# A streaming transformer layer in one kernel: the first stage's products ahead of their norms, the selection norms one head earlier, and the two ends of the down phase reordered

## The chip, the cores and the metric

The kernel runs on one core of one Trainium2 chip. The metric is the device time of one execution in microseconds (us), the median of several runs. Names: PE is the matmul engine (PEld its weight loads), DVE the vector engine, ACT the scalar engine, POOL is GpSimd, SP the engine that issues most loads. "ACTq" and "SPq" are their instruction queues, here the issuing of DMAs.

## The reference, cut to what matters

T = 544 tokens (512 of a prompt, 32 of a running stream), 2048 features. One layer: three mixers share an input projection, a merge follows, then a feed-forward part (PEER) that picks 16 of 16,384 experts in each of 8 heads.

```python
def rmsnorm(x, g):
    xf = x.astype(jnp.float32)
    y = xf * lax.rsqrt(jnp.mean(xf * xf, axis=-1, keepdims=True) + EPS) * g.astype(jnp.float32)
    return y.astype(x.dtype)

def memory_kv(mem, g_mem, w_kv):                 # mem: 256 tokens
    k, v = jnp.split(rmsnorm(mem, g_mem) @ w_kv, 2, axis=-1)
...
gq, gk, gv, gr, ga, sq, sk, sv, mq, gates = in_proj(rmsnorm(x, g_mix), w_in)
...
def peer(h, w_q, g_q, sub_keys, u_tab, v_tab):   # h = rmsnorm(x2, g_ffn)
    q = rmsnorm((x @ w_q).reshape(T, PEER_HEADS, PEER_QDIM), g_q)
    sc = jnp.einsum('thpd,hpkd->thpk', q, sub_keys)
    s_top, i_top = lax.top_k(sc, PEER_TOPK)      # 16 of 128, for both halves
    ...                                          # 16 of the 256 sums; softmax gives the gates
    a = jnp.einsum('td,tkd->tk', xt, u)
    c = gt * jax.nn.gelu(a, approximate=False)
    return jnp.einsum('tk,tkd->td', c, vsel)
...
y = rmsnorm(x2 + peer(...), g_final)
```

## The kernel before

**Numbers in two parts.** PE multiplies in a rounded form of fp32, so each operand is split: `hi`, rounded, and `lo`, what is left. A product is hi x hi + hi x lo + lo x hi, three matmuls for each chunk of 128 features.

**The ring of weight pieces.** Weights come as pieces of 128 x 1024 (512 KB) in the order of use. A ring of four slots (`RING`) holds each piece three times: `w_raw`, loaded by SP (`load_piece`, L188), `w_hi` and `w_lo`, both made by POOL (`split_piece`, L198: a rounding, then a subtraction). PE uses a piece in `use_piece` (L214); `piece_used` frees its slot. SP may load piece i when piece i - 4 is split, POOL split it when piece i - 4 is used.

**Norms.** Activations lie with features on partitions, so a norm's sum of squares is a matmul with a matrix of ones (`Norm.add_square`, L299), after ACT's squares. Then ACT takes the root (`root`), DVE the reciprocal (`invert`) and, for each chunk of 128 features, the product with gain and reciprocal root (L333); ACT rounds it to `hi` and DVE subtracts for `lo` (`scale`, L321).

**Stages.** Each stage is a block of five engine programs, and all engines meet at its end. The first is `stage_memory_kv`: it norms the 256 memory tokens and multiplies them with 32 pieces, two for each of 16 output blocks. Beside them ACT squares x, a chunk a block, and PE sums it. `stage_input_projection` reloads x, scales it, and multiplies it with 117 blocks of two pieces. At the end of a stage POOL splits the four pieces with which the next begins.

**Selection** (`stage_select`). Each of 8 heads has six "up" blocks on PE (`up.tensor`; the products of the experts' first table), which do not depend on the head and fill the time. `up.scalar` evicts them through a Gelu on ACT. Their results alternate between two PSUM banks, and a block may start when the one two before it is evicted. A head itself runs: queries loaded, squared (ACT), summed (PE), root (ACT), reciprocal and two scalings (DVE), one up block meanwhile; 20 score matmuls (PE), copied by ACT; then a long chain on DVE for the 16 best (`max1` ... `idx2`), the 256 candidates (`cand`), the best of these, `over`, ACT's exponential, and `gate`.

**The down phase** (`stage_experts`). 32 sets (`G`), each of four rows of keys. DVE weighs the up results with the gates (`weigh`, L2340), ACT rounds (L2318), DVE subtracts (`rest`, L2345); the terms of a set are prepared during the set before. PE makes 16 blocks (`j`) of a set in four PSUM banks, DVE adds each to `y` in SBUF (L2362). The last 128 tokens are treated apart: POOL gathers a row of the table for each slot and DVE adds it (`add_down`), five to a set. In the last set PE also sums the squares of the finished blocks for the final norm, whose scaled chunks are stored as they come.

## Time and profile before

| | before |
|---|---|
| time, median of 3 runs (lowest to highest) | 5435.06 us (5430.29 to 5442.83) |
| the profiled execution's own time, and its span | 5435.13 us, 5433.3 us |
| granted clock of PE, mean over the span | 0.973 |
| PE matmul busy | 5161.4 us (95%) |
| DVE busy | 2467.3 us (45%) |
| ACT busy | 830.0 us (15%) |
| POOL busy | 3489.8 us (64%) |
| moved by DMA | 1011 MB, 186 GB/s |

The span runs from the first to the last instruction of the profiled execution. The granted clock is the share of PE's full clock of 2.4 GHz that it was given, 0.50 or 1.00 at any moment. Matmuls are pipelined, and a busy PE is not PE at its peak. In a timeline the bracket is the idle time of the engine before the instruction, and what ended it.

### The profile page before, as it was taken

How to read it: one execution, taken by the hardware profiler on the slowest of the kernel's cores; microseconds unless marked ns; L12 is line 12 of the kernel's file. 1: busy time of each engine (PE TensorE's matmuls, PEld its weight loads, DVE VectorE, ACT ScalarE, POOL GpSimd, SP SyncE). 2: the span in 40 equal slices, each digit the busy share in tenths (PEclk: the TensorE clock that was granted, in tenths of full speed). 3: DMA queues.
4: the chain of work that ended last, by engine and by line, in shares of the span. 5: the costliest groups of instructions: out<-in, count | busy, mean ns of one | idle time of the engine just before them, and what ended most of it. 6: DMA issues, size and time to landing. Idle time of an engine off the chain costs nothing. (4 is left out here: it accounts for less than half of the span.)

```text
span 5433.3 us, 90535 instructions
## 1 busy us (share of the span) xinstructions
PE 5161.4 (95%) x33434; PEld 5007.2 (92%) x33434; DVE 2467.3 (45%) x3782; ACT 830.0 (15%) x1318; POOL 3489.8 (64%) x2072
## 2 busy tenths in 40 slices
PE   8899999999999889989999999999998899999998
PEld 8899999999989776989898889999998899999998
DVE  1200000012211243430207777888885788888854
ACT  2100000023322333100101111212211000000001
POOL 7555555544444232555456777888887799999974
PEclk9999999999999989999999999999999999999999
DMA  5333333333232443652323334988897888888852
GB/s 195 130 113 110 109 111 110 117 105 108 83 122 101 146 149 113 214 179 82 119 105 131 122 126 147 327 322 323 323 334 258 318 309 301 311 308 301 301 170 95
DMA packets 344224, 1011.39 MB, mean 186 GB/s; under 512 B 39632, under 2 KB 133680, under 8 KB 308288
## 3 DMA queue, kind: packets, MB, share of 16 engines
...
q14 instruction: 77, 0.63, 0.0%
HBM read 883.11 MB, written 126.76 MB: 186 GB/s over the span
## 5 line engine op out<-in xcount | busy, mean ns | idle before, releaser
L208 POOL TENSOR_TENSOR w_lo<-w_raw,w_hi 128x1024 fp32r<-128x1024 f32 x906 | 2216.9, 2447 | 168.5 <-POOL w_hi L204 167.2
L204 POOL TENSOR_SCALAR w_hi<-w_raw 128x1024 fp32r<-128x1024 f32 x906 | 1003.7, 1108 | 1676.2 <-PE ps L232 1453.5
L228 PE MATMUL ps<-h_hi,w_hi 128*128 128x272 f32 (+1 forms) x6816 | 1740.8, 312 | 85.2 <-DVE h_lo L321 34.5
L232 PE MATMUL ps<-h_hi,w_lo 128*128 128x272 f32 (+1 forms) x6816 | 1718.2, 309 | 0.0
L230 PE MATMUL ps<-h_lo,w_hi 128*128 128x272 f32 (+1 forms) x6816 | 1708.3, 308 | 0.0
L228 PEld LDWEIGHTS ps<-h_hi,w_hi 128*128 128x128 f32 x6816 | 1144.4, 190 | 111.1 <-issue 105.4
L230 PEld LDWEIGHTS ps<-h_lo,w_hi 128*128 128x128 f32 x6816 | 1144.1, 190 | 6.4
L232 PEld LDWEIGHTS ps<-h_hi,w_lo 128*128 128x128 f32 x6816 | 1138.0, 190 | 2.8
L228 PE MATMUL ps<-ex_c_hi,w_hi 128*128 128x416 f32 x2048 | 720.0, 352 | 34.8 <-DVE ex_c_lo L2345 34.5
L232 PE MATMUL ps<-ex_c_hi,w_lo 128*128 128x416 f32 x2048 | 723.7, 353 | 0.0
L230 PE MATMUL ps<-ex_c_lo,w_hi 128*128 128x416 f32 x2048 | 715.7, 349 | 0.0
L1307 DVE SCALAR_TENSOR_TENSOR swa_sb_s<-ps,swa_sb_bias 128x384 f32<-128x384 f32 (+2 forms) x32 | 16.2, 508 | 1191.5 <-PE ps L1156 1191.5
L228 PEld LDWEIGHTS ps<-ex_c_hi,w_hi 128*128 128x128 f32 x2048 | 385.1, 188 | 38.5 <-issue 36.1
L2362 DVE TENSOR_TENSOR ex_y<-ps,ex_y 128x416 f32<-128x416 f32 x512 | 296.4, 584 | 223.6 <-PE ps L232 220.1
L230 PEld LDWEIGHTS ps<-ex_c_lo,w_hi 128*128 128x128 f32 x2048 | 385.5, 188 | 6.6
L232 PEld LDWEIGHTS ps<-ex_c_hi,w_lo 128*128 128x128 f32 x2048 | 384.6, 188 | 2.3
L1850 DVE SCALAR_TENSOR_TENSOR g_sb_u_rows<-g_sb_u_rows,ps 128x2048 f32<-128x2048 f32 x128 | 291.8, 2280 | 118.9 <-DMA g_sb_u_rows<-peer_u,sp_expert 118.8
L1862 DVE SCALAR_TENSOR_TENSOR ps<-ex_v_rows,sp_coef,ps 128x2048 f32<-128x2048 f32 x127 | 297.8, 2345 | 25.5 <-DMA ex_v_rows<-peer_v,sp_expert 25.5
L2175 DVE TENSOR_SCALAR g_sb_rows<-const_sb,sp_turned 128x128 f32<-128x128 f32 x416 | 301.9, 726 | 3.8 <-PEq L1873 3.8
L2318 ACT ACTIVATE ex_c_hi<-ex_c 128x416 fp32r<-128x416 f32 x128 | 70.4, 552 | 1068.9 <-DVE ex_c L2340 972.8
L2345 DVE TENSOR_TENSOR ex_c_lo<-ex_c,ex_c_hi 128x416 fp32r<-128x416 f32 x128 | 206.3, 1613 | 3.4 <-ACT ex_c_hi L2318 3.4
L2340 DVE TENSOR_TENSOR ex_c<-ex_up,ex_gate 128x416 f32<-128x416 f32 x128 | 173.5, 1358 | 25.3 <-DMA ex_gate<-gate 25.3
...
## 6 DMA issues: line engine op xcount, KB each, us to landing
...
up<-up_out ACTq DMA_DIRECT2D x128, 208.0 KB, 3.3
...
```

Source lines behind the costliest of these rows:

```text
L204: pool.tensor_scalar(self.whi[:, slot, :], self.raw[:, slot, :], 1.0, 1.0, ALU.mult, ALU.mult).then_inc(self.hi_done, 1)
L208: pool.tensor_tensor(self.wlo[:, slot, :], self.raw[:, slot, :], self.whi[:, slot, :].bitcast(F32), ALU.subtract).then_inc(self.split_done, 1)
L228: pe.matmul(acc, hi, x, start=first, stop=False)
L230: pe.matmul(acc, hi, x, start=False, stop=False)
L232: mm = pe.matmul(acc, lo, x, start=False, stop=last)
L1850: dve.scalar_tensor_tensor(row_of_slot, row_of_slot, 1.0, self.token_rows, ALU.mult, ALU.mult, accum_out=self.dot[:, s:s + 1]).then_inc(se ...
L1862: dve.scalar_tensor_tensor(self.token_rows, buf[:, s % GATHERS, :], c, self.token_rows, ALU.mult, ALU.add).then_inc(self.summed, 1)
L2175: dve.tensor_scalar(rows[:, group % 2, t, :], iota, of(0), of(2), ALU.is_equal, ALU.mult)
L2318: act.activation(c_hi[:, s, :], c_all[:, c, :], ACT.Copy).then_inc(hi_done, 1)
L2340: dve.tensor_tensor(by_tile(c_all[:, c, :]), by_tile(up[:, parity, c, :]), gate[:, parity, :, c * G_TILE:(c + 1) * G_TILE], ALU.mult).then ...
L2345: dve.tensor_tensor(c_lo[:, VSET * (G % 2) + c, :], c_all[:, c, :], c_hi[:, VSET * (G % 2) + c, :].bitcast(F32), ALU.subtract).then_inc(lo ...
L2362: dve.tensor_tensor(y[:, j, 0:TD], ps[:, 4 + j % 4, 0:TD], y[:, j, 0:TD], ALU.add).then_inc(added, 1)
```

## The change

The memory stage. The operand of the product is the memory times the gain, without the norm; DVE writes it to PSUM, ACT rounds it from there, DVE subtracts. The squares are added up by DVE in PSUM, one matmul with ones sums them over partitions after the third piece, and each output block is multiplied by the reciprocal root when DVE evicts it. The memory is loaded in four parts, with weight piece 0 behind the first. From piece 4 on ACT rounds the weight pieces of this stage, and POOL only subtracts (`rest_of_piece`). The norm of x is made whole in this stage: squares in blocks 0 to 5, the sum after block 6, root and reciprocal in block 7, and two chunks scaled in each of blocks 7 to 14, with x loaded a second time for them. The input projection neither loads nor scales.

Selection. The squares of head h + 1 are made after head h's first up block, summed after its second, the root taken after that; DVE scales the queries between head h's second indices and its candidates; the scores of h + 1 follow head h's sixth up block. Sums and scores of head 0 stand ahead of all up blocks. ACT's exponential of head h moves from behind its fifth eviction to behind its third.

The down phase. Only the first set's terms are loaded at first; SP loads y when they have landed, ACT the next two sets' terms behind its first roundings. The first set's preparation of the second moves to blocks 10 to 14, and the gathers and their adds start one set later. In the last set DVE adds the squares, and PE sums them once, after its last block.

```diff
+    def rest_of_piece(self, pool, slot, i):
+
+        if needed(i - RING + 1):
+            pool.wait_ge(self.piece_used, i - RING + 1)
+        pool.wait_ge(self.hi_done, i + 1)
+        held(pool)
+        pool.tensor_tensor(self.wlo[:, slot, :], self.raw[:, slot, :],
+                           self.whi[:, slot, :].bitcast(F32), ALU.subtract).then_inc(self.split_done, 1)
...
 
...
+        product = lambda b: core.ps[:, 7 if b == 2 else b % 2, 0:N_MEM]
+        tmp = lambda k: core.ps[:, 2 + k % 2, 0:N_MEM]
+        added = total = core.ps[:, 6, 0:N_MEM]
+        sq = lambda k: x[:, k, :]
+        x_sq = lambda k: halves_of(x_part[:, k % (2 * FOUR), :])
+        x_added, x_total, x_rstd = core.acc_view(2), core.acc_view(1), core.acc_view(3)
+        x_tmp = lambda k: core.acc_view(1 + k % 2)
+        x_squares_of = lambda b: range(SQUARES * b, min(SQUARES * (b + 1), KD))
+        x_scaled_of = lambda b: range(2 * (b - X_SCALE), 2 * (b - X_SCALE) + 2) if 0 <= b - X_SCALE < KD // 2 else ()
...
+            part = lambda n: slice(FOUR * n, FOUR * n + FOUR)
+            sp.dma_start(core.gain[:, :], io["gain"]).then_inc(gain_loaded, 16)
+            sp.dma_start(x[:, part(0), :], io["mem"][:, part(0), :]).then_inc(x_loaded[0], 16)
+            core.load_piece(sp, 0, AT_MEM)
+            for n in range(1, KD // FOUR):
+                sp.dma_start(x[:, part(n), :], io["mem"][:, part(n), :]).then_inc(x_loaded[n], 16)
+            for n in range(1, RING):
+                core.load_piece(sp, n, AT_MEM + n)
             sp.dma_start(core.const[:, :], io["const"]).then_inc(core.const_loaded, 16)
-            sp.dma_start(core.gain[:, :], io["gain"]).then_inc(core.const_loaded, 16)
-            core.load_pieces(sp, AT_MEM, AT_IN + RING)
+            core.load_pieces(sp, AT_MEM + RING, AT_IN + RING)
-            core.split_pieces(pool, AT_MEM, AT_IN + RING)
+            core.split_pieces(pool, AT_MEM, POOL_FIRST)
+            for i in range(POOL_FIRST, PIECES_MEM):
+                core.rest_of_piece(pool, i % RING, i)
+            core.split_pieces(pool, AT_IN, AT_IN + RING)
...
+            for b in range(MEM_BLOCKS):
+                if b > 2:
+                    pe.wait_ge(kv_ready, b - 1)
+                for piece in range(2):
+                    i = AT_MEM + 2 * b + piece
+                    core.use_piece(pe, i % RING, i, [
+                        ([product(b)], [hi[:, k, :]], [lo[:, k, :]], k == 0, k == KD - 1,
+                         (lo_ready, k + 1) if b == 0 else None, None)
+                        for k in range(PIECE_K * piece, PIECE_K * (piece + 1))])
+                    if i == AT_MEM + 2:
+                        pe.wait_ge(core.const_loaded, 16)
+                        pe.wait_ge(sq_added, KD)
+                        pe.matmul(total, core.ones, squares[:, :], start=True, stop=True).then_inc(sum_ready, 1)
+                if b == X_SUM:
+                    pe.wait_ge(x_sq_added, KD)
+                    for out, (t0, n) in zip(core.acc(1), HALVES):
+                        mm = pe.matmul(out, core.ones, x_squares[:, t0:t0 + n], start=True, stop=True)
+                    mm.then_inc(sum_ready, 1)
...
+            def round_piece(i):
+                act.wait_ge(core.hi_done, i)
+                act.wait_ge(core.raw_loaded[i % RING], 16 * (i // RING + 1))
+                act.wait_ge(core.piece_used, i - RING + 1)
+                act.activation(core.whi[:, i % RING, :], core.raw[:, i % RING, :], ACT.Copy).then_inc(core.hi_done, 1)
+
+            def square_x(k):
+                n = k // FOUR
+                act.wait_ge(x_part_loaded[n % 2], 16 * (n // 2 + 1))
+                act.activation(x_sq(k), x_sq(k), ACT.Square).then_inc(x_sq_ready, 1)
+            for k in range(KD):
+                act.wait_ge(tmp_ready, k + 1)
+                act.activation(hi[:, k, :], tmp(k), ACT.Copy).then_inc(hi_ready, 1)
+                act.activation(sq(k), x[:, k, :], ACT.Square).then_inc(sq_ready, 1)
+            for b in range(MEM_BLOCKS):
+                for piece in range(2):
+                    if POOL_FIRST <= 2 * b + piece + RING < PIECES_MEM:
+                        round_piece(2 * b + piece + RING)
...
+                    if piece == 0:
+                        for k in x_squares_of(b):
+                            square_x(k)
...
+                        for k in x_scaled_of(b):
+                            act.wait_ge(x_scaled, k + 1)
+                            act.activation(halves_of(h_hi[:, k, :]), x_tmp(k), ACT.Copy).then_inc(x_hi_ready, 1)
...
+                if b == 0:
+                    act.wait_ge(core.const_loaded, 16)
+                    act.wait_ge(sum_ready, 1)
+                    act.activation(std[:, :], total, ACT.Sqrt, bias=core.eps,
+                                   scale=1.0 / D_MODEL).then_inc(std_ready, 1)
+                act.wait_ge(kv_ready, b + 1)
+                act.dma_start(row(io["mem_kv"], b), kv[:, b % 2, :]).then_inc(kv_stored[b % 2], 16)
...
+            for k in range(KD):
+                dve.wait_ge(x_loaded[k // FOUR], 16)
+                if needed(k - 1):
+                    dve.wait_ge(lo_ready, k - 1)
+                dve.tensor_scalar(tmp(k), x[:, k, :], mem_gain(k), None, ALU.mult).then_inc(tmp_ready, 1)
+                if k:
+                    rest(k - 1)
+            rest(KD - 1)
...
+            for k in range(KD):
+                add(k, added, sq(k), squares[:, :], sq_ready, sq_added)
...
+            for b in range(MEM_BLOCKS):
+                for k in x_squares_of(b):
+                    add(k, x_added, x_sq(k), halves_of(x_squares[:, :]), x_sq_ready, x_sq_added)
+                if b == 0:
+                    dve.wait_ge(std_ready, 1)
+                    dve.reciprocal(rstd[:, :], std[:, :]).then_inc(rstd_ready, 1)
+                    dve.wait_ge(rstd_ready, 1)
+                if needed(b // 2):
+                    dve.wait_ge(kv_stored[b % 2], 16 * (b // 2))
+                dve.wait_ge(core.piece_used, AT_MEM + 2 * b + 2)
+                dve.tensor_tensor(kv[:, b % 2, :], product(b), rstd[:, :], ALU.mult).then_inc(kv_ready, 1)
+                if b == X_SCALE:
+                    dve.wait_ge(std_ready, 2)
+                    dve.reciprocal(x_rstd, halves_of(x_std[:, :])).then_inc(rstd_ready, 1)
+                    dve.wait_ge(rstd_ready, 2)
+                for k in x_scaled_of(b):
+                    n = KD // FOUR + k // FOUR
+                    dve.wait_ge(x_part_loaded[n % 2], 16 * (n // 2 + 1))
+                    if needed(k - 1):
+                        dve.wait_ge(x_lo_ready, k - 1)
+                    dve.scalar_tensor_tensor(x_tmp(k), halves_of(x_part[:, k % (2 * FOUR), :]), mix_gain(k), x_rstd, ALU.mult,
+                                             ALU.mult).then_inc(x_scaled, 1)
+                    if k:
+                        x_rest(k - 1)
+            x_rest(KD - 1)
...
-            norm.copies(act)
...
-            norm.scale(dve)
...
-            def head(h):
+            def sums(h):
                 pe.wait_ge(act_s.sem, act_s.at("sq", h))
+            def scores(h):
                 pe.wait_ge(keys_loaded, 16 * (h + 1))
...
-                for n in range(1, UP_HEAD):
+
+            def head(h, last=False):
+                for n in range(2):
                     up.tensor(pe, UP_HEAD * h + n, n)
-            rounds(pe, PEER_HEADS, head)
-
-            pe.wait_ge(dve_s.sem, dve_s.at("gate", PEER_HEADS - 1))
+                if not last:
+                    sums(h + 1)
+                for n in range(2, UP_HEAD):
+                    up.tensor(pe, UP_HEAD * h + n, n)
+                if not last:
+                    scores(h + 1)
+            sums(0)
+            scores(0)
+            rounds(pe, PEER_HEADS - 1, head)
+            head(PEER_HEADS - 1, last=True)
...
+                pair = UP_HEAD // 2 * h
                 if not last:
-
                     load(h + 1)
-                for n in range(1, UP_HEAD - 1):
-                    up.scalar(act, UP_HEAD // 2 * h + n // 2, n % 2)
-                act.wait_ge(dve_s.sem, dve_s.at("over", h))
+                up.scalar(act, pair, 0)
+                if not last:
+                    square(h + 1)
+                up.scalar(act, pair, 1)
+                if not last:
+                    root(h + 1)
+                up.scalar(act, pair + 1, 0)
+                act.wait_ge(dve_s.sem, dve_s.at("over", h) - (normed if last else 0))
                 held(act)
-                act.activation(e[:, :, :], over[:, :, :], ACT.Exp).then_inc(*act_s.did("e"))
-                up.scalar(act, UP_HEAD // 2 * h + (UP_HEAD - 1) // 2, 1)
+                act.activation(e[:, :, :], over[:, :, :], ACT.Exp).then_inc(*(
+                    (act_s.sem, 1) if last else act_s.did("e")))
+                for n in range(3, UP_HEAD):
...
+                if last:
+                    dve_s.skip("rstd", "qn0", "qn1")
+                else:
+                    normalize(h + 1)
...
+    FIRST_ADDS = 1
+    WEIGH_AT = {j: (c,) for c, j in enumerate((0, 2, 4, 6))}
+    REST_AT = {j: (c,) for c, j in enumerate((8, 9, 11, 12))}
+    FIRST_WEIGH_AT, FIRST_REST_AT = {10: (0, 1), 11: (2, 3)}, {13: (0, 1), 14: (2, 3)}
...
         def _(sp):
+            sp.wait_ge(terms_loaded[0], 32)
+            for n in range(4):
+                sp.dma_start(y[:, 4 * n:4 * n + 4, :], rows("x2")[:, 4 * n:4 * n + 4, :]).then_inc(y_loaded[n], 16)
-                while s < SLOTS and (s < GATHERS or add_piece(s - GATHERS) + 2 <= i - AT_DOWN - RING):
+                while s < SLOTS and add_piece(s - GATHERS) + 2 <= i - AT_DOWN - RING:
...
-                    if isinstance(G, int) and G == LAST and piece:
-                        for k in (2 * piece - 2, 2 * piece - 1):
-                            norm.add_square(pe, k, k % 2, k == 0, False)
...
-            for k in (KD - 2, KD - 1):
-                norm.add_square(pe, k, k % 2, False, k == KD - 1)
+            pe.wait_ge(norm.sq_used, KD)
+            for out, (t0, n) in zip(norm.sum, norm.halves):
+                mm = pe.matmul(out, core.ones, squares[:, t0:t0 + n], start=True, stop=True)
+            mm.then_inc(squares_summed, 1)
...
-            for n in range(4):
-                act.dma_start(y[:, 4 * n:4 * n + 4, :], rows("x2")[:, 4 * n:4 * n + 4, :]).then_inc(y_loaded[n], 16)
-            load_terms(1)
+                if G == 0:
+                    load_terms(1)
...
-            norm.scalar(act)
+            act.activation(norm.std[:, 0:1], core.eps, ACT.Sqrt)
+            for k in range(KD):
+                norm.square(act, k)
+            act.wait_ge(squares_summed, 1)
+            norm.root(act)
...
+            def add_square(k):
+                dve.wait_ge(norm.sq_ready, k + 1)
+                if k == 1:
+                    dve.tensor_tensor(squares[:, :], norm.sq[:, 0, :], norm.sq[:, 1, :],
+                                      ALU.add).then_inc(norm.sq_used, 2)
+                    return
+                dve.wait_ge(norm.sq_used, k)
+                dve.tensor_tensor(squares[:, :], squares[:, :], norm.sq[:, k % 2, :],
+                                  ALU.add).then_inc(norm.sq_used, 1)
...
+                    elif j % 4 == 0:
+                        dve.wait_ge(y_loaded[j // 4], 16)
                     dve.tensor_tensor(y[:, j, 0:TD], ps[:, 4 + j % 4, 0:TD], y[:, j, 0:TD],
                                       ALU.add).then_inc(added, 1)
-                    if G < LAST and j in (0, 2, 4, 6):
-                        weigh(G + 1, j // 2)
-                    if G < LAST and j in (8, 9, 11, 12):
-                        rest(G + 1, (8, 9, 11, 12).index(j))
-                    if j % 3 == 1 and s < SLOTS:
+                    if G < LAST:
+                        for c in (WEIGH_AT if G else FIRST_WEIGH_AT).get(j, ()):
+                            weigh(G + 1, c)
+                        for c in (REST_AT if G else FIRST_REST_AT).get(j, ()):
+                            rest(G + 1, c)
+                    elif j >= 2:
+                        add_square(j - 1)
+                    if j % 3 == 1 and s < SLOTS and G >= FIRST_ADDS:
                         sparse.add_down(dve, buf, s)
...
+            add_square(KD - 1)
             norm.vector(dve, out=y)
```

## Rows read from the trace of the kernel before

**Rows 1.** Groups by line, 50 to 146 us: count | busy us, mean ns | idle before

```profile
L208 POOL TENSOR_TENSOR w_lo<-w_raw,w_hi 128x1024 fp32r<-128x1024 f32 x28 | 67.0, 2394 | 5.1 <-POOL w_hi L204 5.1
...
L204 POOL TENSOR_SCALAR w_hi<-w_raw 128x1024 fp32r<-128x1024 f32 x27 | 28.4, 1052 | 0.0
```

**Rows 2.** Timeline of PE, memory stage: start us, duration us, engine, line

```profile
134.00 0.35 PE L228 MATMUL ps<-mem_hi,w_hi 128*128 128x256 f32 x1
...
136.94 1.08 PE L304 MATMUL ps<-in_sq,const_sb 128*128 128x272 f32 x4
```

**Rows 3.** Timeline of the start, POOL and PE

```profile
11.89 1.04 POOL L204 TENSOR_SCALAR w_hi<-w_raw 128x1024 fp32r<-128x1024 f32 x1 [11.44 <-DMA w_raw<-weights]
...
27.44 0.55 PE L228 MATMUL ps<-mem_hi,w_hi 128*128 128x256 f32 x1 [4.64 <-DVE mem_lo L321]
```

**Rows 4.** Timeline from the memory stage into the input projection

```profile
146.17 1.16 PE L304 MATMUL ps<-in_sq,const_sb 128*128 128x272 f32 x4 [0.94 <-ACT in_sq L466]
...
152.91 2.34 POOL L208 TENSOR_TENSOR w_lo<-w_raw,w_hi 128x1024 fp32r<-128x1024 f32 x1 [0.18 <-POOL w_hi L204]
...
155.55 2.04 SPq L498 DMA_DIRECT2D in_x<-x  x4
...
163.00 0.79 PE L228 MATMUL ps<-h_hi,w_hi 128*128 128x272 f32 x2 [15.68 <-DVE h_lo L321]
...
188.44 0.63 ACT L537 ACTIVATE in_stage<-ps 128x544 f32<-128x544 f32 x1 [2.02 <-PE ps L232]
```

**Rows 5.** Timeline of selection, ACT and PE

```profile
2869.78 0.52 ACT L1813 ACTIVATE up_out<-ps 128x416 f32<-128x416 f32 x1 [8.54 <-PE ps L232]
...
2900.85 3.97 PE L1917 MATMUL ps<-sel_sb_sq,const_sb 128*128 128x272 f32 x8 [4.00 <-ACT sel_sb_sq L1953]
...
2914.77 2.58 PE L1927 MATMUL ps<-sel_sb_keys,sel_sb_qn 128*128 128x128 f32 x20 [0.44 <-DVE sel_sb_qn L2000]
```

**Rows 6.** The score matmuls, by their line

```profile
L1927 PE MATMUL ps<-sel_sb_keys,sel_sb_qn x160: 272/275/348, 2848.8 to 3313.5; 128*128 128x128 f32 x128, 128*32 128x128 f32 x32
```

**Rows 7.** Timeline of selection, DVE, one head

```profile
2984.97 2.03 DVE L2006 MAX8 sel_sb_top<-sel_sb_sc 128x8 f32<-128x128 f32 x10 [4.36 <-ACT sel_sb_sc L1965]
...
2997.42 1.47 DVE L2028 TENSOR_TENSOR sel_sb_cand<-sel_sb_top 128x1280 f32<-128x1280 f32 x1
...
3010.97 5.98 DVE L2072 TENSOR_TENSOR sel_sb_hot<-sel_sb_rank,const_sb 128x1280 f32<-128x1280 f32 x2
...
3026.66 0.77 DVE L2093 TENSOR_TENSOR sel_sb_chosen<-sel_sb_e,sel_sb_inv 128x80 f32 x1 [0.24 <-DVE sel_sb_inv L2090]
...
3039.49 3.55 DVE L1995 RECIPROCAL sel_sb_rstd<-sel_sb_std 128x544 f32<-128x544 f32 x1 [12.06 <-ACT sel_sb_std L1956]
```

**Rows 8.** Timeline of the start of the down phase

```profile
4204.24 9.52 ACTq L2310 DMA_DIRECT2D ex_y<-x  x1
...
4224.31 2.10 DVE L2340 TENSOR_TENSOR ex_c<-ex_up,ex_gate 128x416 f32<-128x416 f32 x4 [22.64 <-DMA ex_gate<-gate]
...
4232.22 0.69 PE L228 MATMUL ps<-ex_c_hi,w_hi 128*128 128x416 f32 x1 [34.49 <-DVE ex_c_lo L2345]
```

**Rows 9.** There: us; busy PE, PEld, DVE, ACT, POOL; clock; DMA; GB/s

```profile
4210.00:4220.00 10.00, 0.00 (x0) 0.00 (x0) 0.00 (x0) 0.00 (x0) 0.00 (x0) 0.50 1.02 414
```

**Rows 10.** Timeline of DVE in the last set

```profile
5406.77 0.59 DVE L2362 TENSOR_TENSOR ex_y<-ps,ex_y 128x416 f32<-128x416 f32 x1 [3.52 <-PE ps L232]
...
5409.04 0.59 DVE L2362 TENSOR_TENSOR ex_y<-ps,ex_y 128x416 f32<-128x416 f32 x1 [1.68 <-PE ps L232]
```

**Rows 11.** Groups of instructions by line, DVE, whole span

```profile
L2362 DVE TENSOR_TENSOR ex_y<-ps,ex_y 128x416 f32<-128x416 f32 x512 | 296.4, 584 | 223.6 <-PE ps L232 220.1 <-issue 1.8
...
L2345 DVE TENSOR_TENSOR ex_c_lo<-ex_c,ex_c_hi 128x416 fp32r<-128x416 f32 x128 | 206.3, 1613 | 3.4 <-ACT ex_c_hi L2318 3.4
...
L2000 DVE SCALAR_TENSOR_TENSOR sel_sb_qn<-sel_sb_q,gain_sb,sel_sb_rstd 128x544 f32<-128x544 f32 x16 | 27.2, 1740 | 1.9 <-DVE sel_sb_rstd L1995 1.9
...
L1859 DVE TENSOR_SCALAR ps<-ex_v_rows,sp_coef 128x2048 f32<-128x2048 f32 x1 | 2.3, 2339 | 0.0
```

243 lines of the change are left out of this document (122 added, 121 removed).

## The prediction

> **What bounds the kernel now.** The page comes first: the matmul engine (PE) is busy for 95% of the span, so only its idle stretches, its stretches at the low clock, and the one stage in which its "busy" hides a wait are worth anything. I then read the clock and busy time by stretches, and after that the timelines of the four places that the diff touches. An edit is worth what it does to PE, or to what follows PE's last matmul.
>
> The start is poor: up to 27.4 us PE has no product to work on [rows 3], and it stands again between 147.3 and 163 [rows 4]. While it stands it is granted 0.50 of 2.4 GHz [rows 9]. Between them PE reads as full, but one piece of 24 matmuls takes 2.94 us (134.00 to 136.94), and four sums of squares of 1.08 together follow every second piece [rows 2]. GpSimd (POOL) needs 2.39 + 1.05 + 0.18 = 3.62 us for a piece [rows 1], against PE's 2.94 + 0.54. So in the memory stage POOL is the bound.
>
> **Part 1, the memory stage.** Now PE's first product starts at 27.4, though the first weights had landed by 11.9 [rows 3]. After the change the product needs no norm: DVE multiplies by the gain, ACT rounds, DVE subtracts, and the norm divides the product later. The transfers ahead of weight piece 0 fall from 2.7 MB to 0.6 MB; 3.2 MB had landed by 11.9, so 1.1 MB should land by about 6 (an estimate), and POOL's 3.6 us put PE's start near 9.8. But POOL splits the first four pieces alone (ready near 10, 16, 19, 23, as pieces 1 to 3 queue behind three parts of x), and ahead of its fourth piece PE waits for the sum of squares: 16 operand chunks at about 0.85 us a chunk, then 16 dependent additions at 0.55 each, an estimate from 0.58 for 416 elements [rows 11]. That ends at 7.9 + 13 + 8.8 = 29.6. From there 29 pieces at 2.92 are 84.7; I add 2.5 for matmuls at the low clock, 0.8 for the second sum and 1.4 for a stall at block 7, where DVE inverts the second root (3.55 for such a reciprocal [rows 7]) ahead of the copies that hold ACT's next rounding. The stage's last piece ends at 119. Now it ends at 147.3 [rows 4].
>
> POOL's part of a piece falls to 2.6, ACT's rounding is about 1.0 more, and both lie behind PE: a freed slot has three pieces (8.8 us) until it is wanted. In blocks 7 to 14 ACT rounds the odd piece only after two copies that wait for DVE, about 3.5 us after PE ends the block: 3.5 + 1.0 + 2.6 = 7.1, so 1.7 us of cover is left. If that goes, each such block costs what it lacks. DVE's new work has a PSUM operand everywhere, and such work does not stretch beside POOL: 0.58 us for 416 elements with one input in PSUM, but 1.61 with both in SBUF [rows 11].
>
> **Part 2, into the input projection.** Now x is reloaded and scaled here, and block 0 is evicted at 188.4 [rows 4]. POOL ends at 155.25, the next stage's first DMA goes at 155.55 [rows 4]: the boundary itself costs some 0.3 us. After, PE finds its operands ready, but POOL must still split the four pieces that the next stage begins with. Piece 31 leaves POOL about 4.5 us before PE's end, and four times 3.6 later POOL is done 9.8 us behind it. Block 0 is then out at 119 + 10.2 + 12.0 (this stage's block) + 2.4 (low clock) = 143.6. Parts 1 and 2 save 188.4 - 143.6 = **45**; bounds 34 (the loop of ring slots loses 11) and 53 (sum and boundary each cheaper by 4). The eight loads of x stay eight, now all on ACT's queue. The wait for the stored keys moves to the end of SP's queue, where nothing stands behind it.
>
> **Part 3, selection.** At each of seven head boundaries PE sits idle for 4.00 us until ACT has squared the next queries, and then works at the low clock, 3.97 us for 8 sums [rows 5]; the same kind of sums at full clock cost 3.52 - 1.68 = 1.84 [rows 10]. The pitch of a head is (3313.5 - 2.4 - 2848.8)/7 = 66.0, from the first and the last start of the score matmuls [rows 6], of which a head's 20 take 2.5 to 2.6 [rows 5]. Without the wait it is six blocks of 0.52 + 8.54 = 9.06 [rows 5], 1.84 for the sums and 2.5 for the scores: 58.7. Seven heads save 51. Head 0 pays: its block 0 used to cover the chain root, reciprocal, two scalings, and now follows it; 3.55 [rows 7], two scalings of 0.8 beside an idle POOL to 1.74 on average [rows 11] and some 0.7 for the root make about 6.5, with 1 for the clock. Net 44.
>
> What is late next? DVE has 12.45 us from its first maximum to the candidates, 13.55 from there to "over", and 15.7 + 0.8 on to the gates [rows 7]. Counted from the end of a head's scores, DVE finishes the second indices at 14.0 and waits for the next root until 22.1 (two blocks, the sums, a Gelu, a table load, the root); reciprocal and scalings end at 29.5, "over" at 43.1, the gates at 59.5. The next head's scores are ready for DVE at 60.3, so DVE keeps up by 0.8. ACT now waits for "over" before it may evict block 3: exponential and two table loads later this is out at 46.6, and PE wants that bank for block 5 at 47.2. A margin of 0.6 us on seven heads: I charge 1 in all. **Part 3: 43**; bounds 25 (each head loses 2.5) and 46.
>
> **Part 4, start of the down phase.** ACT issues the first terms at about 4204 and then stands 9.5 us on one load of y; DVE gets the terms at 4224.3, PE starts at 4232.2 after 34.5 idle [rows 8]. Now nothing but the first terms (1.7 MB) is in flight: y waits for them, the gathered rows come a set later. At the 414 GB/s that the queues moved then [rows 9] they are 4.1 us; with the start of a transfer and the gates' short runs I take 7, an estimate, so 4211, and 4.6 for four weighings and four remainders beside free engines: PE at 4215.6, 16.6 earlier. SP's y now stands ahead of weight pieces 4 to 7: by PE's need of piece 4 (7 + 3 x 4.5 later, 4236) some 11 MB must have moved, about what this rate gives (13 in 32 us); I charge 1.5. And set 1's weighings come two at blocks 10 and 11, its remainders two at 13 and 14: 0.58 + 2 x 1.61 = 3.8 a block [rows 11] against PE's 2.27, so DVE is 3 us late when PE wants set 1. **Part 4: 12**; bounds 4 and 17.
>
> **Part 5, the last norm.** The last set loses seven pairs of sums on PE at 1.84 each (the wait before the add alternates 3.52, 1.68 [rows 10]): **13**. DVE adds the squares instead, 15 of them under PE's 2.27 a block, with four banks of slack. These additions have two SBUF inputs. I take no stall on PE, as a set has so far held eight such instructions (1.61 for a remainder) and five gathered additions without one. Behind the last add, one addition more against a table load less: zero, within 1. Bounds 9 and 14.
>
> A rule of the Trainium skill bears on this (SBUF — State Buffer, "Who interferes with whom"): a DVE instruction with two SBUF inputs contends with a GpSimd instruction that reads SBUF, and the later one waits for all of the other. The trace agrees: 1.61 against 0.58 [rows 11]. By the rule the eight or so additions beside POOL's last pieces would each wait up to 2.4, and the sum would lose at most 3 of the 13.
>
> Sum: 45 + 43 + 12 + 13 = 113. The profiled execution took 5435.1 (span 5433.3 and 1.8 around it), and the median of the runs is 5435.06: **5322**.
>
> **Rivals.** (a) ACT's wait for "over" costs PE 2 to 3 us a head and its clock as well: 18 to 20 back, **5341**. For it: the margin of 0.6; against: DVE's times repeat well.
> (b) The loop of slots fails in the first stage, ACT's copies holding back the rounding: 8 blocks at 1.5, and POOL's last four pieces later too: **5336**.
> (c) y and terms 1 and 2 starve PE of weights in the first set: part 4 falls to nothing, **5334**. For it: the DMA engines are the bound there.
> (d) The gain multiplication contends with POOL after all: it reads SBUF alone. Sixteen instructions that wait a mean 1.2 put the sum of squares 15 to 19 later: **5339**. Against: the one such instruction with its result in PSUM took 2.34 for 2048 elements beside POOL's work [rows 11], an element a cycle with no wait. The Trainium skill (VectorE: DVE Perf Modes, "Why PSUM operands drop a tier") says that any PSUM operand bars the two-port mode; the trace agrees.
> (e) Slower: DVE becomes selection's bound. If the eight wide DVE instructions of a head each wait a whole subtraction of POOL's (2.4) more than now, the pitch grows by 19: 7 x 19 - 113 = +20, **5455**. It decides from 16 us a head. Against: these instructions were measured beside POOL already; only the scalings move.
>
> **Numbers.** Forecast 0.55, (a) 0.15, (b) 0.10, (c) 0.08, (d) 0.05, (e) 0.02, and 0.05 for two of (a) to (d) together, which would end near 5360. About 0.2%, 11 us, is what a measurement of this kernel can tell from no change. The low bounds of all parts give 5435 - 34 - 25 - 4 - 9 = 5363, the high ones 5435 - 53 - 46 - 17 - 14 = 5305. The range is 5300 to 5365. Faster 0.96, same 0.01, slower 0.03.
>
> **What would show it.** After: PE's first product near 10 with a wait of some 6 us before its fourth piece; the memory stage's last piece near 119 and POOL idle in it; block 0 evicted near 144; heads at a pitch of 59 and no wait for the squares; DVE idle some 8 us before the reciprocal; PE restarting 18 us after its last up block; the last set free of sums. Wrong would be a pitch over 61, a memory stage of over 3.1 us a piece, or a wait for weights in the first down set.

## The result, and the profile after

The changed kernel takes 5340.3 us (median of 4 runs, 5333.5 to 5347.0) against 5436.8 for the kernel before on the same chip; the ratio is 0.9812, interval 0.9800 to 0.9824, so 96 to 109 us less. Forecast was 5322. Two executions, both of the run with the three edits together, took longer (5423.3 and 10176.1 us) and are left out of its median. The profiled execution has a span of 5338.1 against 5433.3, 95.2 less. Its page says of the engines:

```profile
PE 5102.9 (96%) x33252; PEld 4964.4 (93%) x33252; DVE 2513.0 (47%) x3845; ACT 848.1 (16%) x1331; POOL 3462.1 (65%) x2044
```

PE's busy time falls by 58 us, the sums of squares among it; the other 37 were idle. The work itself, weight pieces and experts, is unchanged, and so the way to read the change is stretch by stretch between events that both traces have:

| from, to | before, us | after, us | saved | forecast |
|---|---|---|---|---|
| start, first eviction of the input projection | 188.4 | 142.1 | 46.3 | 45 |
| on to selection's first sum of squares | 2646.6 | 2646.6 | 0.0 | 0 |
| selection, to the first transposition of the gates stage | 529.6 | 493.0 | 36.6 | 43 |
| gates stage, to the last up eviction | 833.2 | 842.4 | -9.2 | 0 |
| on to the first add of down set 1 | 75.3 | 65.4 | 9.9 | 12 |
| sets 1 to 30 | 1090.8 | 1090.3 | 0.5 | 0 |
| last set, first add to last add | 45.1 | 34.0 | 11.1 | 13 |
| last add to the end | 24.3 | 24.4 | -0.1 | 0 |

**The start.** Timeline of the start (start us, us, engine, line; in brackets the idle time before and its releaser), which answers to [rows 3]:

```profile
7.14 1.04 POOL L217 TENSOR_SCALAR w_hi<-w_raw 128x1024 fp32r<-128x1024 f32 x1 [6.70 <-DMA w_raw<-weights]
...
11.01 0.55 PE L250 MATMUL ps<-mem_hi,w_hi 128*128 128x256 f32 x1 [11.01 <-DVE mem_lo L538]
```

Weight piece 0 is there at 7.1, not at 11.9, and PE starts at 11.0, not at 27.4. The sum of squares comes after the third piece:

```profile
28.85 0.42 DVE L554 TENSOR_TENSOR mem_squares<-ps,mem_x 128x256 f32<-128x256 f32 x1
...
29.42 1.19 PE L474 MATMUL ps<-mem_squares,const_sb 128*128 128x256 f32 x2 [5.34 <-DVE mem_squares L554]
```

It starts at 29.42, which was forecast as 29.6, and PE stands 5.3 us for it. PE's last piece of the stage ends at 117.6 (127.87, the next stage's first matmul, less 10.28 of waiting), and POOL's fourth split of the next stage's pieces ends at 127.2. This answers to [rows 4].

**Selection.** The timeline of ACT in one head, which answers to [rows 5]:

```profile
2884.60 0.72 ACT L2069 ACTIVATE sel_sb_std<-ps,const_sb 128x544 f32<-128x544 f32 x1
...
2893.68 0.52 ACT L1909 ACTIVATE up_out<-ps 128x416 f32<-128x416 f32 x1
...
2907.46 1.28 ACT L2095 ACT_TABLE_LOAD   x1 [13.26 <-DVE sel_sb_over L2198]
2908.76 0.27 ACT L2095 ACTIVATE sel_sb_e<-sel_sb_over 128x80 f32<-128x80 f32 x1
2909.04 1.28 ACT L1909 ACT_TABLE_LOAD   x1
2910.34 0.52 ACT L1909 ACTIVATE up_out<-ps 128x416 f32<-128x416 f32 x1
...
2911.79 0.52 ACT L1909 ACTIVATE up_out<-ps 128x416 f32<-128x416 f32 x1 [0.94 <-ACT up_out L1909]
```

The root is taken at 2884.6, between the second and the third eviction. PE does not wait for it; DVE does, 8.37 us in this head (next rows), which the prediction expected ("some 8 us"). Then ACT stands 13.3 us for DVE's "over", loads two tables around the exponential, and evicts block 3 only at 2910.34. Block 4 is evicted right behind it. What DVE did in that time (answers to [rows 7]):

```profile
2885.55 3.55 DVE L2119 RECIPROCAL sel_sb_rstd<-sel_sb_std 128x544 f32<-128x544 f32 x1 [8.37 <-ACT sel_sb_std L2069]
...
2892.87 2.33 DVE L2160 TENSOR_TENSOR sel_sb_cand<-sel_sb_top 128x1280 f32<-128x1280 f32 x1
...
2906.27 1.08 DVE L2198 TENSOR_TENSOR sel_sb_over<-sel_sb_best 128x80 f32<-128x80 f32 x1
2907.28 5.08 DVE L2204 TENSOR_TENSOR sel_sb_hot<-sel_sb_rank,const_sb 128x1280 f32<-128x1280 f32 x2
```

"cand" takes 2.33 where it took 1.47, and "over" ends at 2907.35, 44.1 us after the copy of the head's scores begins (2863.23). The 2.33 is no scatter: "cand" took 1.47 in all eight heads before, and 2.32 or 2.33 in the first seven heads after. What differs is POOL's rounding of a weight piece. Before, it begins with "cand" or up to 0.1 us behind it, and it is POOL's rounding that takes longer (1.05 alone):

```profile
2997.43 2.38 POOL L204 TENSOR_SCALAR w_hi<-w_raw 128x1024 fp32r<-128x1024 f32 x1 [0.96 <-PE ps L232]
```

After, it begins 0.3 to 0.4 us ahead of "cand" (here at 2892.51 against 2892.87) and "cand" takes longer, and so does POOL's subtraction that follows (2.40 alone):

```profile
2892.51 1.35 POOL L217 TENSOR_SCALAR w_hi<-w_raw 128x1024 fp32r<-128x1024 f32 x1 [0.84 <-PE ps L254]
2894.04 3.42 POOL L221 TENSOR_TENSOR w_lo<-w_raw,w_hi 128x1024 fp32r<-128x1024 f32 x1 [0.18 <-POOL w_hi L217]
```

And on PE, between block 4 and block 5:

```profile
2910.06 0.35 PE L254 MATMUL ps<-h_hi,w_lo 128*128 128x416 f32 x1
2911.26 0.42 PE L250 MATMUL ps<-h_hi,w_hi 128*128 128x416 f32 x1 [0.84 <-POOL w_lo L221]
```

PE idles 0.84 us, and the start of block 5 is 1.0 us late against the 0.19 between its matmuls. The row names a weight piece of POOL as the releaser. The copies of the scores are 59.9 us apart from the second head on (2863.23, 2923.12, ...). The granted clock stays at 1.00 through all of these heads.

**The gates stage.** Nothing in it was edited. DVE's timeline near its start:

```profile
3293.04 2.29 DVE L1946 SCALAR_TENSOR_TENSOR g_sb_u_rows<-g_sb_u_rows,ps 128x2048 f32<-128x2048 f32 x1 [9.69 <-DMA g_sb_u_rows<-peer_u,sp_expert]
...
3296.42 1.84 DVE L2310 TENSOR_SCALAR g_sb_cols<-const_sb,sp_turned 128x128 f32<-128x128 f32 x1
3298.17 0.33 DVE L2309 TENSOR_SCALAR g_sb_rows<-const_sb,sp_turned 128x128 f32<-128x128 f32 x1
3298.43 2.43 DVE L2310 TENSOR_SCALAR g_sb_cols<-const_sb,sp_turned 128x128 f32<-128x128 f32 x1
```

DVE makes four one-hot pairs, a group, then waits for the first gathered rows of the table, multiplies them, and makes the next group. Two instructions that take 0.28 us elsewhere take 1.84 and 2.43 here, while POOL rounds and subtracts a piece (3297.10 to 3300.78). PE stands 5.23 us for that group:

```profile
3301.01 2.05 PE L2291 MATMUL ps<-g_sb_cols,g_sb_rows 128*128 128x128 f32 x8 [5.23 <-DVE g_sb_cols L2310]
```

**The down phase.** DVE's timeline from the first terms on (answers to [rows 8]):

```profile
4137.03 2.10 DVE L2485 TENSOR_TENSOR ex_c<-ex_up,ex_gate 128x416 f32<-128x416 f32 x4 [9.14 <-DMA ex_gate<-gate]
4139.04 2.09 DVE L2490 TENSOR_TENSOR ex_c_lo<-ex_c,ex_c_hi 128x416 fp32r<-128x416 f32 x4
4145.96 0.59 DVE L2516 TENSOR_TENSOR ex_y<-ps,ex_y 128x416 f32<-128x416 f32 x1 [4.83 <-PE ps L254]
...
4169.13 3.46 DVE L2485 TENSOR_TENSOR ex_c<-ex_up,ex_gate 128x416 f32<-128x416 f32 x2
...
4180.88 3.56 DVE L2490 TENSOR_TENSOR ex_c_lo<-ex_c,ex_c_hi 128x416 fp32r<-128x416 f32 x2
```

The terms arrive at 4137.0 and PE starts at 4141.4, after 17.5 us idle instead of 34.5. But two weighings of set 1 begin at 4169.1, the last two remainders end at 4184.4, and PE waits for them:

```profile
4184.89 0.69 PE L250 MATMUL ps<-ex_c_hi,w_hi 128*128 128x416 f32 x1 [5.04 <-DVE ex_c_lo L2490]
```

**The end**, which answers to [rows 10]:

```profile
5313.74 0.59 DVE L2516 TENSOR_TENSOR ex_y<-ps,ex_y 128x416 f32<-128x416 f32 x1 [1.04 <-PE ps L254]
...
5315.89 1.28 PE L2436 MATMUL ps<-ex_squares,const_sb 128*128 128x272 f32 x4 [2.19 <-DVE ex_squares L2499]
...
5317.95 3.55 DVE L338 RECIPROCAL last_rstd<-last_std 128x544 f32<-128x544 f32 x1 [2.12 <-ACT last_std L312]
```

The adds come every 2.27 us up to the last, within 0.05; one sum of 1.28 follows.

### The profile page after: what moved, and what is told of

It reads as the page before. It is cut to its first block and busy times, and to the rows that moved or that the text cites. A ratio compares the mean times of both kernels' runs of the same rounds, so it can differ in the third digit from the quotient of the medians.

```text
span 5338.1 us, 89996 instructions
## 1 busy us (share of the span) xinstructions
PE 5102.9 (96%) x33252; PEld 4964.4 (93%) x33252; DVE 2513.0 (47%) x3845; ACT 848.1 (16%) x1331; POOL 3462.1 (65%) x2044
## 3 DMA queue, kind: packets, MB, share of 16 engines
q10 hardware_dynamic: 142640, 215.86, 11.4%
## 5 line engine op out<-in xcount | busy, mean ns | idle before, releaser
L221 POOL TENSOR_TENSOR w_lo<-w_raw,w_hi 128x1024 fp32r<-128x1024 f32 x878 | 2157.8, 2458 | 163.4 <-POOL w_hi L217 160.9
L217 POOL TENSOR_SCALAR w_hi<-w_raw 128x1024 fp32r<-128x1024 f32 x878 | 967.9, 1102 | 1598.6 <-PE ps L254 1353.6
L2309 DVE TENSOR_SCALAR g_sb_rows<-const_sb,sp_turned 128x128 f32<-128x128 f32 x416 | 315.7, 759 | 12.0 <-PEq L1969 12.0
L637 ACT ACTIVATE in_stage<-ps 128x544 f32<-128x544 f32 x73 | 45.7, 626 | 835.0 <-PE ps L254 835.0
```

Source lines behind the costliest of these rows:

```text
L217: pool.tensor_scalar(self.whi[:, slot, :], self.raw[:, slot, :], 1.0, 1.0, ALU.mult, ALU.mult).then_inc(self.hi_done, 1)
L221: pool.tensor_tensor(self.wlo[:, slot, :], self.raw[:, slot, :], self.whi[:, slot, :].bitcast(F32), ALU.subtract).then_inc(self.split_done, 1)
L637: act.activation(halves_of(stage[:, u, :]), core.acc_view(u), func).then_inc(out_ready, 1)
L2309: dve.tensor_scalar(rows[:, group % 2, t, :], iota, of(0), of(2), ALU.is_equal, ALU.mult)
```

## The experiments

Times of whole runs scatter by some 10 us on either side of a median, so small effects are read from the stretches of the profiled executions and the ratios stand beside them. Each group of four ran on one chip with the kernel before, whose medians were 5446.0, 5445.2 and 5442.8.

### The exponential behind the fifth eviction

```diff
                 up.scalar(act, pair + 1, 0)
+                for n in range(3, UP_HEAD - 1):
+                    up.scalar(act, pair + n // 2, n % 2)
                 act.wait_ge(dve_s.sem, dve_s.at("over", h) - (normed if last else 0))
...
-                for n in range(3, UP_HEAD):
-                    up.scalar(act, pair + n // 2, n % 2)
+                up.scalar(act, pair + (UP_HEAD - 1) // 2, 1)
```

> The changed kernel with one edit: in each head of selection ACT's exponential stands behind the fifth eviction again (it waits for "over" there), not behind the third. Theory A (ACT's wait for "over" makes the eviction of a head's fourth up block late, so PE loses about 1.1 us a head at its sixth up block): the 0.84 us wait of PE in each head goes, the pitch of a head falls from 59.9 to 58.8 us, seven heads give 8 us, about 5332. Rival B (the row says what it means: POOL's weight piece is late there): the wait stays, pitch 59.9, 5340. Rival C (the exponential is then late for DVE's sum): DVE waits for it before the gates and the next head's maxima slip, pitch over 60.

Measured: 5331.6, ratio 0.9795 (0.9770 to 0.9821). Selection takes 485.7 instead of 493.0, 7.3 less, and the copies of the scores are 59.1 and 58.8 apart. ACT's timeline in the same head:

```profile
2900.56 0.52 ACT L1909 ACTIVATE up_out<-ps 128x416 f32<-128x416 f32 x1 [7.27 <-PE ps L254]
...
2909.62 0.52 ACT L1909 ACTIVATE up_out<-ps 128x416 f32<-128x416 f32 x1 [8.55 <-PE ps L254]
...
2910.91 1.28 ACT L2097 ACT_TABLE_LOAD   x1 [0.77 <-ACT up_out L1909]
2912.21 0.27 ACT L2097 ACTIVATE sel_sb_e<-sel_sb_over 128x80 f32<-128x80 f32 x1
...
2921.59 1.03 ACT L2077 ACTIVATE sel_sb_sc<-ps 128x1024 f32<-128x1024 f32 x1 [1.11 <-DVE sel_sb_inv L2223]
```

Block 3 is evicted at 2900.56, as soon as PE has made it, and PE has no idle time in the head. POOL's work was not touched, so the releaser in PE's row was the wrong name: it was ACT's late eviction (theory A). ACT's copy of the scores now waits for DVE's last work on the head (the 1.11 in the last row). But DVE still idles 7.9 us in each head before its reciprocal, and that takes the lateness up: a head of 58.8 us is PE's own work without a gap, near the 58.7 of the prediction.

### The first dot product one group later

```diff
-                for _ in range(DOTS_AFTER[group % STEPS]):
+                for _ in range(DOTS_AFTER[group % STEPS] if group else 0):
```

> The changed kernel with one edit: in the gates stage the first gathered dot product stands behind DVE's second group of one-hot rows, not behind its first. Theory A (PE's 5.2 us wait at the second group comes from DVE's order: that group stands behind a dot product that waits 9.7 us for the first gathered rows, and is then stretched beside POOL): the wait goes and with it some 2 us at the low clock; last up block less first transposition falls from 842.3 to about 835, total 5333. Rival B (the gathered rows and the shared DMA engines bound the start of the stage): the wait moves to the third group with much the same size, 842, 5340.

Measured: 5336.2, ratio 0.9796 (0.9776 to 0.9817). The gates stage takes 827.0, 15 less than after the change (7 were expected) and 6 less than before it, and the view of waits has none of PE for one-hot columns in it. The middle of the kernel, which no edit touches, took 12 us more in this execution, which hides it in the total. Theory A holds for the wait, at twice its price in this pair of executions, of which the changed one had a late landing (the table below).

### The weighings of set 1 earlier

```diff
-    FIRST_WEIGH_AT, FIRST_REST_AT = {10: (0, 1), 11: (2, 3)}, {13: (0, 1), 14: (2, 3)}
+    FIRST_WEIGH_AT, FIRST_REST_AT = {7: (0,), 8: (1,), 9: (2,), 10: (3,)}, {11: (0,), 12: (1,), 13: (2,), 14: (3,)}
```

> The changed kernel with one edit: in the first down set the four weighings of set 1 stand at blocks 7 to 10 and its remainders at 11 to 14, one a block, instead of two at 10, 11, 13, 14. Theory A (the 5.0 us wait of PE before set 1 is DVE's order alone): the wait goes and the 2 us at the low clock behind it, set 1 starts 7 us earlier, 5333. Rival B (the terms of set 1 have not landed at block 7, about 25 us after PE's start): DVE waits for the transfer, the adds to y behind it are late and PE stalls for a bank in the first set: no gain or a loss of up to 5 us, 5340 to 5345.

Measured: 5339.4, ratio 0.9809 (0.9789 to 0.9828). Set 1 ends 5.1 us earlier (72.9 against 78.0 from the first add to set 1's last), but the last set begins 1.5 us later (1135.3 against 1133.8 from the first add). The view of waits over the down phase (waiting engine and operation, releaser: us, times, longest), here:

```profile
DVE ps L1958 <- DMA ex_v_rows<-peer_v,sp_expert: 60.5, 44, 6.2
...
PE ps L250 <- DVE ex_c_lo L2490: 18.7, 2, 17.4
...
PE ps L250 <- DVE ex_y L2516: 4.6, 4, 2.1
```

and in the changed kernel:

```profile
PE ps L250 <- DVE ex_c_lo L2490: 22.5, 2, 17.5
DVE ps L1958 <- DMA ex_v_rows<-peer_v,sp_expert: 20.7, 22, 2.6
```

The terms had landed, so rival B is out, and the wait before set 1 falls from 5.0 to 1.3 (each total has the 17.5 of the start in it). The gain is gone by set 16: DVE waits 60 us for gathered rows instead of 21, and PE four times, 4.6 us, for a bank that DVE has not emptied. Whether the edit does this is not shown. The run with SBUF operands (below) has the down phase of the changed kernel, and there too DVE waited 65.3 us for gathered rows, and PE for banks.

### The three edits together

> The three edits of the other runs together on the changed kernel. Theory: the three losses are separate, each in its own stretch, so their gains add: 8 + 7 + 7 = 22 us, 5318. Rival: the start of the gates stage depends on when selection ends, so that part comes out otherwise beside the first edit; then the sum misses by the size of that wait, 5 us.

Measured: 5313.8 (5310.1 to 5327.1, the three executions that the ratio takes), ratio 0.9756 (0.9731 to 0.9781), against 0.9812 (0.9800 to 0.9824) for the changed kernel. The profiled execution is one of the two left out (its gates stage took 926 us), so its stretches are not read. By the two ratios the edits together give 30 us, and by the ends of their intervals 10 to 51: they help, but the expected 22 and the rival's 5 less can't be told apart.

### Each part alone

The kernel before, with functions of the changed one: `stage_memory_kv` and `stage_input_projection`; `stage_select`; `stage_experts` with only the start changed; `stage_experts` with only the last norm changed.

```diff
-            norm = Norm(core, norm_ctx, "in", None, KD, T, G_MIX, hi, lo, 4, core.sem("in_x_loaded"))
-            stage_memory_kv(core, norm)
-            stage_input_projection(core, hi, lo, norm)
+            stage_memory_kv(core, hi, lo, kv, kv_stored)
+            stage_input_projection(core, hi, lo, kv_stored)
```

> The kernel before with the memory stage and the input projection of the change alone. Theory A (the parts are independent, and the first stage gives all of its 46.3 us by block 0 of the input projection): block 0 evicted at 142, 46 us less than before, and every later stage as long as before. Rival B (the gain is given back, since the stages behind it start with other timings): less than 40 in the total while block 0 is at 142.

Measured: 5395.6, ratio 0.9895 (0.9876 to 0.9913). The first eviction comes at 143.4, 45.0 earlier; the unchanged middle took 8 us more in this execution. By the ratio the part gives 47 to 67 us, by its own stretch 45; nothing is seen to be given back (theory A).

> The kernel before with the selection of the change alone. Both theories: selection itself (first sum of squares to the gates stage's first transposition) falls from 529.6 to 493.0 us, with a PE wait of about 0.85 in each of seven heads. Theory A (the 9.5 us longer gates stage of the changed kernel was chance of that execution): the gates stage takes about 833 us to its last up block, total 36 less. Rival B (selection's new end makes the start of the gates stage wait): gates stage 842, PE waits 5 us for the second group, total 27 less.

Measured: 5407.1, ratio 0.9929 (0.9912 to 0.9946), span 5396.2. Selection 492.6, gates stage 835.4: theory A, 37 less.

> The kernel before with the start of the down phase of the change alone, the last norm as before. Theory: PE restarts 17.5 us after its last up block instead of 34.5, then waits 5 us before set 1 and works 2 us more at the low clock: 17.0 - 7.2 = 10 less in total. Rival (the later gathered adds end beyond their old place and cost what the start gives): sets 24 to 30 longer by some us, less than 5 in total.

Measured: 5429.9, ratio 0.9967 (0.9954 to 0.9979). PE's first down product stands 17.2 us behind the start of the last up eviction instead of 34.4, and from there to the first add of the last set it is 1140.2 instead of 1131.7: 17.1 - 8.5 = 8.6 less, near the 10 expected. The ratio says more, 11 to 25 us.

> The kernel before with the last norm of the change alone. Theory A (six pairs of sums leave the last set, the seventh ran behind PE's last block anyway): last set's adds 45.1 us apart from first to last before, 34.0 after, total 11.1 less. Rival B (the seventh pair counts too, as forecast): 13 less, tail 1.8 shorter.

Measured: 5430.1, ratio 0.9976 (0.9963 to 0.9989). The last set takes 36.3 from last add to last add instead of 47.4, 11.1 less (theory A).

By their own stretches the four parts give 45.0, 37.0, 8.6 and 11.1, together 101.7, and the whole change gave 96 to 109. By the medians of the ratios they would give 57, 39, 18 and 13, which is 127. So the ratios of this group are some 25 us too kind in sum, for no reason that the runs show, and the stretches are to be believed.

### The changed kernel again, and with two of the edits

> The changed kernel once more, unaltered, for the scatter of its stages. Theory A (the length of the gates stage hangs on when the first gathered rows land): if DVE's first dot product begins 11 us or more behind the stage's first transposition, PE waits 5 to 6 us for the second group and the stage takes 842 to 844 us; if it begins at 10.5 or before, the wait is at most 2 and the stage takes 833 to 837. Rival B (the changed kernel's gates stage is longer by itself): 842 or more with an early landing too.

Measured: 5341.9, ratio 0.9819 (0.9803 to 0.9836). All executions with the unaltered order at the start of the gates stage, by how long after the first transposition the first dot product begins:

| execution | dot product at, us | PE's wait for the group | gates stage |
|---|---|---|---|
| before | 9.5 | none | 833.2 |
| only the down start | 10.0 | 2.0 | 836.5 |
| SBUF operands (below) | 10.0 | 0.5 | 833.8 |
| earlier weighings | 10.0 | 0.4 | 833.6 |
| only the last norm | 10.1 | 0.5 | 837.0 |
| only the first stage | 10.3 | none | 834.9 |
| only selection | 10.5 | 1.8 | 835.4 |
| changed, again | 11.0 | 2.4 | 837.2 |
| POOL rounds (below) | 11.3 | 2.8 | 837.5 |
| changed | 11.4 | 5.2 | 842.4 |
| exponential later | 12.1 | 5.9 | 844.1 |

The same changed kernel gave 842.4 and 837.2, so rival B (842 or more in any case) is out, and of the 9.2 us lost in the stage about half is the chance of that execution. A late landing goes with a long stage, but theory A has its limits wrong: at 11.3 and 11.4 the wait was 2.8 and 5.2. In the second of these POOL's piece held up two instructions of the group (1.84 and 2.43 us), in the first one (1.65), so it matters as well what POOL does at that moment. Whether the rows land later on average after the new selection is open: the landings past 10.5 are all of kernels with it, but two such kernels are at 10.0 and one at 10.5.

The last run has the edits of the first two experiments together (diffs above).

> The changed kernel with the exponential behind the fifth eviction and the first dot product behind the second group, the down phase as in the change. Theory: selection 485.7, gates stage 827 whenever the rows land; together 7.3 from selection and 6 to 15 from the gates stage, so 13 to 22 less than the changed kernel beside it, about 5322. Rival: in the gates stage the wait only moves to a later group in this combination: 7 less.

Measured: 5324.3 (5320.1 to 5331.5), ratio 0.9784 (0.9767 to 0.9800), against 5341.9 and 0.9819 for the changed kernel beside it: 17.6 us less. Selection 485.9, gates stage 827.1, with the rows used from 11.8 on. This version is ahead of both kernels.

### What the first stage owes to each step

```diff
-    FOUR, SQUARES, X_SUM, X_SCALE, POOL_FIRST = 4, 3, 6, 7, RING
+    FOUR, SQUARES, X_SUM, X_SCALE, POOL_FIRST = 4, 3, 6, 7, PIECES_MEM
...
-            for i in range(POOL_FIRST, PIECES_MEM):
-                core.rest_of_piece(pool, i % RING, i)
```

> The changed kernel, but POOL rounds and subtracts every piece of the memory stage itself; ACT rounds none. Theory A (without ACT's rounding POOL is the stage's bound again at 3.6 us a piece): PE's last piece ends about 10 us later, near 127, and block 0 of the input projection is evicted near 152 instead of 142; total 10 more, 5350. Rival B (PE's 2.9 a piece bounds the stage anyway, the pace before came from the sums of squares on PE): block 0 stays at 142.

Measured: 5353.9, ratio 0.9839 (0.9823 to 0.9856), 12 more than the changed kernel beside it. PE's last piece ends at 128.3, block 0 is out at 155.0. The view of PE's waits in the first 170 us:

```profile
PE ps L250 <- POOL w_lo L221: 15.9, 10, 11.3
PE ps L250 <- PEq L413: 11.6, 1, 11.6
PE ps L472 <- DVE mem_squares L552: 5.3, 1, 5.3
```

Without the 11.3 at the start, nine waits for POOL of 4.6 us remain, and more of POOL's pace is hidden in a slow PE (0.45 to 0.57 before each of the last pieces, 3.6 us apart). Theory A.

```diff
-        tmp = lambda k: core.ps[:, 2 + k % 2, 0:N_MEM]
-        added = total = core.ps[:, 6, 0:N_MEM]
+        m_tmp, xs_tmp, xs_rstd = sb("m_tmp", [P, 2, N_MEM]), sb("xs_tmp", [P, 2, T]), sb("xs_rstd", [P, T])
+        tmp = lambda k: m_tmp[:, k % 2, :]
+        added, total = squares[:, :], core.ps[:, 6, 0:N_MEM]
...
-        x_added, x_total, x_rstd = core.acc_view(2), core.acc_view(1), core.acc_view(3)
-        x_tmp = lambda k: core.acc_view(1 + k % 2)
+        x_added, x_total, x_rstd = halves_of(x_squares[:, :]), core.acc_view(1), halves_of(xs_rstd[:, :])
+        x_tmp = lambda k: halves_of(xs_tmp[:, k % 2, :])
```

> The changed kernel, but in the memory stage the products of gain and memory, the running sums of squares, the scaled chunks of x and x's reciprocal root stand in SBUF instead of PSUM. Theory A (DVE's instructions with all operands in SBUF wait for POOL's subtractions, as the remainders of the down phase do with 1.6 us against 0.6): the chain up to the sum of the memory's squares, 29.4 now, ends some 8 us later, and the second half of the stage loses its cover too; last piece at 125 or later instead of 117.6, total 8 to 20 more. Rival B (POOL's reads do not hold these short instructions up): each takes 0.4 to 0.5 us as now, the last piece at 118, total the same.

Measured: 5372.7, ratio 0.9876 (0.9858 to 0.9894), 31 more than the changed kernel beside it. DVE's groups by line in the first 130 us, with SBUF (two of the four kinds of tensor that moved):

```profile
L555 DVE TENSOR_TENSOR mem_x_squares<-mem_x_squares,mem_x_part 128x544 f32<-128x544 f32 x15 | 28.1, 1874 | 11.9 <-ACT mem_x_part L497 10.9
...
L544 DVE TENSOR_SCALAR mem_m_tmp<-mem_x,gain_sb 128x256 f32<-128x256 f32 x16 | 14.5, 913 | 7.1 <-DMA mem_x<-mem 5.6
```

and in the changed kernel, with PSUM:

```profile
L554 DVE TENSOR_TENSOR ps<-ps,mem_x_part 128x544 f32<-128x544 f32 x14 | 10.3, 733 | 11.3 <-ACT mem_x_part L496 10.2
L543 DVE TENSOR_SCALAR ps<-mem_x,gain_sb 128x256 f32<-128x256 f32 x16 | 7.7, 487 | 7.2 <-DMA mem_x<-mem 5.7
```

A running sum of x's squares takes 1.87 us in place of 0.73, a product with the gain 0.91 in place of 0.49. SBUF by itself is not slow. The timeline of DVE in the same run has both, a product before POOL has begun or between its instructions and one beside POOL's subtraction (8.72 to 11.21):

```profile
6.95 0.35 DVE L544 TENSOR_SCALAR mem_m_tmp<-mem_x,gain_sb 128x256 f32<-128x256 f32 x1
...
9.12 2.25 DVE L544 TENSOR_SCALAR mem_m_tmp<-mem_x,gain_sb 128x256 f32<-128x256 f32 x1
...
11.80 0.35 DVE L544 TENSOR_SCALAR mem_m_tmp<-mem_x,gain_sb 128x256 f32<-128x256 f32 x1
```

A running sum of x's squares, too, takes 0.72 us while POOL is idle (41.8 and 42.6 us) and up to 2.73 beside it. The memory's sum of squares starts at 41.5 instead of 29.4, PE waits 7.8 us for evictions that DVE has not come to and 10.0 for pieces, and the stage's last piece ends at 153.0. Theory A, but beyond its 8 to 20: DVE, busy for 65.0 of the first 150 us in the changed kernel, is here busy for 119.2, and the other engines wait for it. The Trainium skill (SBUF — State Buffer, "Who interferes with whom") has the rule that a DVE instruction with two SBUF inputs contends with a GpSimd instruction that reads SBUF, and one with at most one SBUF input outside the two-port modes does not; this pair of runs agrees. The product has one SBUF input and waited as well, so the rule covers it only if it ran in a two-port mode. For that speaks that it takes 0.35 us undisturbed in SBUF, and 0.49 with its result in PSUM.

## Why the prediction was right, and where its sizes were off

The direction and the range held; the time came out 18 us above the forecast. It is within a microsecond of rival (a)'s 5341, but that is chance: (a)'s mechanism accounts for 6 of the 18 us beyond the 1 that was charged, and most of the rest lies in a stage for which no rival was named.

- **Part 1 and 2, 45 forecast, 46.3 measured** (45.0 alone; 42.5 to 45.0 in the seven other executions that have the stage unaltered, which evict block 0 at 143.4 to 145.9). PE started at 11.0 instead of 9.8, because piece 0 landed at 7.1 and not at 6. The sum of squares (29.6 against 29.4) came as worked out in part by luck: the chain began at 5.7 and not at 7.9, and its 16 chunks took 0.92 us each and not 0.85 (with 0.85 the sum's 13 is 13.6). The last piece came at 117.6 (119 forecast); the stall behind block 7 was one wait of 1.2. The rival of the ring's loop did not happen. That ACT's rounding carries it was shown: without it the stage's last piece ends at 128.3, against 117.6 to 120.9 in the executions with it. Rival (d), that DVE contends with POOL, did not happen: the products took 0.49 us each beside POOL, with their results in PSUM. With these and three other kinds of operand in SBUF the kernel took 31 more; the sum of squares, which (d) put 15 to 19 later, then came 12 later.
- **Part 3, 43 forecast, 36.6 measured.** The step "I charge 1 in all" for ACT's wait for "over" was mis-sized. The forecast had block 3 out at 46.6 and PE wanting its bank at 47.2; it was out at 47.6 and wanted at 47.2. The 1.0 is DVE's: the sum went by a "cand" of 1.47, and it took 2.33 in each of the seven heads. Against rival (a) the prediction said that DVE's times repeat well. They did, but at another value, as the new order puts "cand" behind the start of POOL's rounding and not ahead of it. A margin of 0.6 was less than this one stretch of 0.86. Seven heads came to a pitch of 60.2 and not 58.7, 10 us in all, of which 7.3 are this wait: without it the pitch is 59.1. Rival (a) was right in its mechanism and charged two and a half times too much (18 to 20 us); the clock, which it charged too, did not fall. The prediction's "DVE keeps up by 0.8" was no limit either, as DVE idles some 8 us a head. Head 0's exposed chain was 4.7 and not 7.5, which gave 3 back: 10.3 us from its first sum to its scores and 8.1 more behind the last scores (61.6 to the first transposition, 53.5 before), against 13.7 from sum to scores before.
- **Part 4, 12 forecast, about 10 measured** (8.6 alone). PE restarts 17.0 earlier (16.6 forecast). The 1.5 for weights behind y was nothing: PE waited for no weight piece. DVE was 5.0 late for set 1, not 3, and PE lost 2 more at the low clock behind that wait (7.2 of loss up to set 1's first add, 5.0 of it waiting), which the sum left out. Rival (c) is out.
- **Part 5, 13 forecast, 11.1 measured.** The step "seven pairs" was wrong: the seventh pair starts at 5408.8 in the trace of before, with PE's last block done, and ran beside the last add [rows 10], where it cost nothing. Six pairs of 1.85 are 11.1. The additions beside POOL's last pieces were held up, seven of them taking 1.16 to 1.88 us against 0.71 for the rest, but PE lost nothing by it. The tail was zero, as said.
- **The gates stage, nothing forecast, 9.2 lost.** The prediction named no term for it. The experiments split this: up to 5 us is the scatter between two executions of the same kernel; the rest, and whether the new selection moves it, is not settled.

So of the 18 us, 9 are in a stage that the sum passed over, 6 in selection, 2 in the down start and 2 in the count of pairs, less 1 gained at the start.
